# Scores of two attention kinds: bias and mask added by VectorE in the operation that finds the maximum, instead of by TensorE

## The chip, the cores and the metric

The kernel runs on one core of a Trainium2 chip. The metric is the time of one execution in microseconds (us), the median of three runs. Apart from those runs, one execution was profiled; every duration below is from that one.

## What is computed

Two transformer blocks, one after the other, on 256 tokens of width 2048, all in float32. The second block's attention has three kinds of heads, eight of each:

```
diff:  s = q.k * 64**-0.5 - slope[h] * |i - j|, masked by chunks of 64      (two maps for each head)
       w = softmax(s of map 0) - lam * softmax(s of map 1);  o = w v
stick: stick-breaking weights (no softmax)
band:  s = q.k * 64**-0.5 + rel_table[h, clip(i - j)], masked by chunks of 64;  o = softmax(s) v
```

The change touches the scores of the diff heads and of the band heads, and nothing else. The slopes are 2^-1 to 2^-8, one for each diff head.

## The kernel before

**The stream of weights.** Every weight matrix comes in blocks of 128x128, eight to a sub-unit of 512 KB ("sub"). SyncE loads a sub into one of four `raw` buffers (L447), ScalarE rounds it to fp32r into one of five `whi` buffers (L830), VectorE subtracts to make the rest, `wlo` (L1227). TensorE then multiplies each block twice: `whi` with 512 columns (activations as high and low half) and `wlo` with 256. Buffers are given back by semaphores: `sub_done` (TensorE) frees a `whi` buffer, `wlo` (VectorE) frees a `raw` buffer.

**The order.** Four blocks make a "slot"; there are 1860. Everything that is no weight product is a "side task": a generator on each engine, which steps once in each slot, so that the order of every engine's queue is fixed when the program is built. TensorE steps its side tasks after every fourth block. `tasks()` places a diff head (`dfa`, its scores and weights; `dfb`, its output) every 7 slots while the K and the next Q weights stream (v = first slot of stage `ka`: `dfa` h at v+9+7h), and a pair of band heads (`bnd`) at v+117, 127, 135, 143. `BANKS` says in which slots a task holds one of four PSUM banks and which semaphore frees it; `bank_table()` deals them out.

**A diff head before** (`dfa`). TensorE starts both banks (one for each map) with `Ir` x `Dr`, an identity times the table of distances and masks of 384 columns in fp32r, then adds Q x K on top: 128 and 256 columns for each of the two maps, 64 rows deep, in float32, which the trace records as two weight loads and two matmuls each. VectorE takes the maximum of each part (L1458, 128 and 256 columns) and scales it (L1460). ScalarE takes the exponential out of PSUM into SBUF (L1011), with the sum as an accumulator output. VectorE divides and combines the maps (L1463 to L1472, `dif_w`); TensorE transposes three tiles (L649), and `dfb` multiplies with V.

**A pair of band heads before** (`bnd`). TensorE starts each bank with `J` x `hk`: a flip matrix times the head's bias (`HK`), whose rows a DMA read with overlap from a scratch tensor in DRAM, in float32, 128 and 256 columns for each head; then Q x K; then `Ir` x `MCr` in fp32r, the mask of 2 x 64 columns. VectorE's maximum is L1528, ScalarE's exponential L1079, the division L1533 to L1536 (`bnd_w`), the transposes L727.

**The scratch tensor.** In the first block's feed-forward stage, ScalarE's queue loads `c2` (tables) and the 8 rows of the bias, VectorE pads the rows, ScalarE's queue writes the 8 rows of 512 floats to `rel_rows` in DRAM (L985), and after diff head 7 it reads them back as 128 rows of 8 x 256 floats (L1034). ScalarE waits for the write's end before diff head 0, since the diff heads reuse its source.

The lines that follow are of the functions that the change touches.

Of the kernel before, what the change touches and what calls it, by code (L numbers as in the profile page):

```python
# [34 lines left out]
C2 = [("bd", 128), ("tri2", 128), ("flip", 128), ("nm", 384), ("cm", 384), ("dist", 384), ("mc", 64), ("lam", 256)]  # L35
C2_KEPT = 1152
# [173 lines left out]
for _t, _kind, _i in TASKS:  # L210
# [19 lines left out]
    "dfa": [("s0", 2, 5, "dif_exp", 2, 1), ("s1", 2, 5, "dif_exp", 2, 2), ("t", 8, 9, "dif_copy", 1, 1)],  # L230
# [3 lines left out]
    "bnd": [("s0", 2, 6, "bnd_exp", 2, 1), ("s1", 2, 6, "bnd_exp", 2, 2), ("t0", 9, 11, "bnd_copy", 2, 1),  # L234
# [65 lines left out]
def idle(n):  # L300
    for _ in range(n):
        yield
# [3 lines left out]
    "pe_own act_own dve_own pool_own raw0 raw1 raw2 raw3 x0 x1 x2 x3 x4 x5 x6 x7 c1 raw_first whi_first wlo_first scaled vec mem c2 rel rows hank out "  # L306
# [13 lines left out]
class Chip:  # L320


    def __init__(self, nc, ctx, d, out):
# [36 lines left out]
        self.Dr, self.MCr = CR[:, 0:384], CR[:, 384:448]  # L360
# [78 lines left out]
def sync_program(e, c):  # L439
    s = Seq(e, c.sems, "pe_own")  # L440

    def load(w):

        name, i = ORDER[w // 2]
        if w >= NRAW:
            s.wait_ge("wlo", w - NRAW + 1)
        e.dma_start(c.raw[:, w % NRAW, :], c.d[name][i][:, (w % 2) * SUB:(w % 2 + 1) * SUB]).then_inc(c.sems[f"raw{w % NRAW}"], 16)  # L447

    def load_x(i):
        e.dma_start(c.xt(2 * i, 2), c.d["x"][:, 16 + 2 * i * T:16 + (2 * i + 2) * T]).then_inc(c.sems[f"x{i}"], 16)  # L450
# [23 lines left out]
    s.wait_ge("hank", 16)  # L474


def tensor_program(e, c):
# [151 lines left out]
    def dfa(h):  # L629
        yield from idle(2)  # L630
        Q, K = c.Q["a"], c.K["a"]
        p.wait_ge("lam_v", 2)
        p.wait_ge("qk", 10 + 2 * (h // 2))
        banks = [take("dfa", h, f"s{n}") for n in range(2)]
        for bank in banks:
            mm(bank[:, 0:384], c.Ir, c.Dr, True, False)
        for n, bank in enumerate(banks):
            lo, hi = 64 * n, 64 * n + 64
            mm(bank[:, 0:128], Q[lo:hi, h * T:h * T + 128], K[lo:hi, h * T:h * T + 128], False, False)
        for n, bank in enumerate(banks):  # L640
            lo, hi = 64 * n, 64 * n + 64
            p.then_inc(mm(bank[:, 128:384], Q[lo:hi, h * T + 128:(h + 1) * T], K[lo:hi, h * T:(h + 1) * T], False, True),
                       "dif_s")
# [58 lines left out]
    def bnd(i):  # L702
        P0, P1, q = c.bnd[i]
        Q, K, V, J = c.Q["c"], c.K["c"], c.V["c"], c.const2("flip")
        yield from idle(2)
        p.wait_ge("hank", 16)
        p.wait_ge("qk", 30 + 2 * (i // 2))
        banks = [take("bnd", i, f"s{n}") for n in range(2)]
        for n, bank in enumerate(banks):
            hk = c.HK[:, (2 * i + n) * T:(2 * i + n + 1) * T]  # L710
            mm(bank[:, 0:128], J, hk[:, 128:256], True, False)
            mm(bank[:, 128:384], J, hk, False, False)
        for n, bank in enumerate(banks):
# [89 lines left out]
def scalar_program(e, c):  # L803
# [194 lines left out]
    def dfa(h):  # L998
        st = c.SM[:, 16 + 16 * h:32 + 16 * h]
        yield from idle(4)  # L1000
        for n in range(2):
            load(LN_EXP)
            Pb, bank = c.dif[h % 4][n], c.bank("dfa", h, f"s{n}")
            a.wait_ge("dif_max", 2 * h + n + 1)
            if h >= 4:
                a.wait_ge("y_made", made("ao", h - 4))
            else:
                a.wait_ge("norm_ok", 5)
                a.wait_ge("rows", 16)
            for o, w, i in ((0, 128, 0), (128, 256, 1)):  # L1010
                a.then_inc(e.activation(Pb[:, o:o + w], bank[:, o:o + w], ACT.Exp, bias=st[:, 2 * n + i:2 * n + i + 1],  # L1011
                                        scale=SLOPES[h], accum_out=st[:, 4 + 2 * n + i:5 + 2 * n + i]),
                           "dif_exp" if i else None)
        yield from idle(5)
        a.wait_ge("dif_turn", h + 1)
        a.then_inc(e.activation(c.dif[h % 4][0][:, 0:384], c.bank("dfa", h, "t")[:, 0:384], ACT.Copy), "dif_copy")
        yield

    def dfb(h):
# [6 lines left out]
        a.wait_ge("lam_v", 4)  # L1026
# [40 lines left out]
    def bnd(i):  # L1067
# [3 lines left out]
        for n, Pb in enumerate((P0, P1)):  # L1071
            st, bank = c.SM[:, 96 + 16 * (2 * i + n):112 + 16 * (2 * i + n)], c.bank("bnd", i, f"s{n}")
            if i:
                a.wait_ge("y_made", made("ao", 8 + i))
            else:
                a.wait_ge("dif_pv", 8)
# [125 lines left out]
def vector_program(e, c):  # L1202
# [183 lines left out]
    def const(_):  # L1386
# [6 lines left out]
        v.then_inc(e.tensor_copy(c.MCr, c.const2("mc")), "lam_v")  # L1393
# [28 lines left out]
        v.then_inc(e.tensor_copy(g8[:, 319:511], g8[:, 318:319].to_broadcast([8, 192])))  # L1422
        v.then_inc(e.tensor_copy(g8[:, 511:512], g8[:, 318:319]), "fill")
# [26 lines left out]
    def dfa(h):  # L1450
# [3 lines left out]
        for n in range(2):  # L1454
            bank = c.bank("dfa", h, f"s{n}")
# [388 lines left out]
def layout(a):  # L1844
# [71 lines left out]
```

## Time and profile before

| | |
|---|---|
| median of 3 runs | 2743.03 us (2742.43 to 2743.47) |
| the profiled execution | 2743.26 us, of which its span is 2741.3 us |
| TensorE busy | 2717.2 us, 99% of the span |
| VectorE busy | 1949.9 us, 71% |
| ScalarE busy | 1284.8 us, 47% |
| granted TensorE clock, mean | 0.998 |
| DMA | 499 MB, mean 182 GB/s |

Busy is time in which an engine executes; a matmul's record overlaps that of the next one, so a single matmul's cost is best read from one start to the next start. L481 is the helper that issues nearly all matmuls, so they are told apart by tile: `H` or `Y` with `whi` or `wlo` are weight products, `CR` holds `Ir`, `Dr` and `MCr`, and `AR` holds nearly everything else.

### The profile page before, as it was taken

The page shows a single profiled execution, that of the slowest core. Times are in us where ns is not written, and L with a number is a line of the kernel's source. Part 1 is how long each engine was busy: PE and PEld are TensorE (multiplying, and loading weights), DVE is VectorE, ACT ScalarE, POOL GpSimd, SP SyncE. Part 2 cuts the span into 40 slices and gives each one's busy share as a digit, 9 for nine tenths or more (in the row PEclk, how much of TensorE's full clock was granted, in tenths as well). Part 3 has the DMA queues.
Part 4 walks back from the last instruction along what each step waited for, and adds up shares of the span by engine and source line. Part 5 has one row for each costly group of instructions (what it writes and reads, how often), then busy time and mean ns, then how long its engine had stood idle before and what let it go on. Part 6 is the DMA issues. An engine that isn't in the chain of part 4 may idle for free.

```text
span 2741.3 us, 39113 instructions
## 1 busy us (share of the span) xinstructions
PE 2717.2 (99%) x16174; PEld 2378.5 (87%) x16174; DVE 1949.9 (71%) x2378; ACT 1284.8 (47%) x1634; POOL 94.7 (3%) x69
## 2 busy tenths in 40 slices
PE   8999999999999999999999999999999999999998
PEld 7888999888898888888888888888988888888886
DVE  7777777876768665666566886776777757775775
ACT  5444455754545443344344554545544433443444
POOL 1000000011101000000000110000100000000001
PEclk9999999999999999999999999999999999999999
DMA  6555555446555555555555555454455555555553
GB/s 240 191 185 185 175 164 173 145 160 223 182 169 189 187 191 194 191 190 189 190 185 193 191 183 170 150 168 144 164 183 185 200 190 178 193 199 190 187 192 124
DMA packets 138192, 499.07 MB, mean 182 GB/s; under 512 B 15248, under 2 KB 16280, under 8 KB 137888
## 3 DMA queue, kind: packets, MB, share of 16 engines
q1 hardware_dynamic: 136224, 491.67, 54.2%
q10 hardware_dynamic: 1792, 4.91, 0.5%
q8 instruction: 127, 2.08, 0.3%
q14 instruction: 49, 0.40, 0.0%
HBM read 494.41 MB, written 2.11 MB: 181 GB/s over the span
## 4 chain that ended last, share of the span: by engine, by line
PE 98%; DVE 1%; DMA 1%; ACT 0%; POOL 0%; issue 0%; DVEq 0%; ACTq 0%; POOLq 0%
PE PS L481 97%; DMA raw<-in_w_in 0%; DVE wlo L1227 0%; POOL AR L1738 0%; ACT whi L830 0%; DMA XG<-in_x 0%; DVE XG L1677 0%; DVE XG L1210 0%; PE PS L573 0%; DVE H L1221 0%; PE PS L727 0%; PE PS L649 0%; ACT AR L837 0%; PE PS L616 0%; DVEq L1785 0%
## 5 line engine op out<-in xcount | busy, mean ns | idle before, releaser
L481 PE MATMUL PS<-H,whi 128*128 128x512 f32 (+1 forms) x5472 | 1788.9, 381 | 8.7 <-DVE wlo L1705 7.9
L1227 DVE TENSOR_TENSOR wlo<-raw,whi 128x1024 fp32r<-128x1024 f32 x929 | 1127.7, 1231 | 638.5 <-ACT whi L830 634.5
L481 PE MATMUL PS<-H,wlo 128*128 128x256 f32 x5072 | 1412.6, 278 | 0.0
L830 ACT ACTIVATE whi<-raw 128x1024 fp32r<-128x1024 f32 x929 | 969.5, 1057 | 921.2 <-PE PS L481 883.2
L481 PEld LDWEIGHTS PS<-H,whi 128*128 128x128 f32 x5472 | 1001.8, 188 | 220.7 <-issue 8.8
L481 PEld LDWEIGHTS PS<-H,wlo 128*128 128x128 f32 x5072 | 956.3, 189 | 3.5 <-issue 3.1
L481 PE MATMUL PS<-Y,whi 128*128 128x512 f32 (+1 forms) x2240 | 719.0, 376 | 1.1 <-DVE XG L1677 0.8
L481 PE MATMUL PS<-Y,wlo 128*128 128x256 f32 x2048 | 569.3, 278 | 0.0
L481 PEld LDWEIGHTS PS<-Y,whi 128*128 128x128 f32 x2240 | 407.8, 188 | 84.0 <-DVE XG L1677 2.0
L481 PEld LDWEIGHTS PS<-Y,wlo 128*128 128x128 f32 x2048 | 385.6, 188 | 0.5 <-issue 0.2
L1549 DVE TENSOR_REDUCE AR<-PS 128x512 f32<-128x1024 f32 x140 | 171.6, 1225 | 14.6
L1738 POOL TENSOR_TENSOR AR<-AR 128x512 f32<-128x512 f32 x48 | 70.5, 1470 | 2003.8 <-ACT AR L837 2002.8
L815 ACT ACTIVATE AR<-AR 128x512 f32<-128x512 f32 x64 | 40.5, 633 | 211.8 <-DVE AR L1237 138.4
L481 PE MATMUL PS<-whi,H 128*128 128x512 f32 (+1 forms) x384 | 105.0, 361 | 0.0
L1210 DVE TENSOR_TENSOR AR<-AR 128x512 f32<-128x512 f32 x114 | 78.9, 692 | 34.7 <-ACT AR L815 32.3
L481 PE MATMUL PS<-AR 128*128 128x256 f32 (+8 forms) x580 | 99.4, 354 | 2.8 <-ACT AR L837 2.2
L1144 ACT ACTIVATE Y<-AR 128x512 fp32r<-128x512 f32 x44 | 27.8, 632 | 150.0 <-DVE AR L1666 150.0
L1237 DVE SCALAR_TENSOR_TENSOR AR<-AR 128x255 f32<-128x255 f32 (+2 forms) x192 | 92.9, 484 | 6.8
L481 PEld LDWEIGHTS PS<-AR 128*128 128x128 f32 (+3 forms) x580 | 61.5, 170 | 22.4 <-issue 11.6
L481 PEld LDWEIGHTS PS<-whi,H 128*128 128x128 f32 x384 | 67.0, 189 | 10.3 <-issue 1.0
L1219 DVE TENSOR_TENSOR Y<-AR,Y 128x512 fp32r<-128x512 f32 (+1 forms) x68 | 42.7, 628 | 37.4 <-ACT Y L1144 34.5
L481 PE MATMUL PS<-wlo,H 128*128 128x512 f32 (+1 forms) x192 | 68.2, 355 | 0.0
(173 smaller groups left out, 895.6 us busy)
## 6 DMA issues: line engine op xcount, KB each, us to landing
raw<-in_ffn SPq DMA_DIRECT2D x528, 512.0 KB, 4.1
raw<-in_w_in SPq DMA_DIRECT2D x177, 512.0 KB, 4.5
raw<-in_w_qkv SPq DMA_DIRECT2D x96, 512.0 KB, 3.7
raw<-in_w_out SPq DMA_DIRECT2D x64, 512.0 KB, 4.2
raw<-in_w_o SPq DMA_DIRECT2D x40, 512.0 KB, 3.6
raw<-in_w_q SPq DMA_DIRECT2D x8, 512.0 KB, 3.9
raw<-in_w_k SPq DMA_DIRECT2D x8, 512.0 KB, 4.3
raw<-in_w_v SPq DMA_DIRECT2D x8, 512.0 KB, 4.6
```

What stands on the lines that cost most here:

```text
L481: return e.matmul(out, l, r, start=start, stop=stop)
L815: return e.activation(dst, src, ACT.Silu)
L830: a.then_inc(e.activation(c.whi[:, s % NW, :], c.raw[:, s % NRAW, :], ACT.Copy), "whi")
L1144: a.then_inc(e.activation(c.hi("Y", 2 * (j - 8 * part), 2), two(q), ACT.Copy), "y_hi")
L1210: return e.tensor_tensor(two(dst), two(src), both(r), ALU.mult)
L1219: v.then_inc(e.tensor_tensor(c.lo(op, k, n), src, hi, ALU.subtract), made_)
L1227: v.then_inc(e.tensor_tensor(c.wlo[:, s % NW, :], c.raw[:, s % NRAW, :], c.whi[:, s % NW, :].bitcast(F32), ALU.subtract), "wlo")
L1237: v.then_inc(e.scalar_tensor_tensor(dst[:, sh:T], src[:, 0:T - sh], taps(width - 1 - sh), dst[:, sh:T], ALU.mult, ALU.add), name if sh == ...
L1549: v.then_inc(e.tensor_reduce(two(dst), c.acc[b].rearrange("p m (h t) -> p m t h", h=2), AX, ALU.add), f"acc{b}", turn + 1)
L1738: g.then_inc(e.tensor_tensor(c.SUM, c.SUM, c.SQ[i % 2], ALU.add), "sum_add")
```

## The change

In both kinds of heads TensorE now makes Q x K alone. VectorE adds the table and finds the maximum in one `tensor_tensor_reduce`: it reads the bank and the table in SBUF, adds, multiplies by -slope (or -1), writes the negated scores to SBUF and gives out their minimum. For the diff heads the table is the same rounded `Dr`, read as float32; for the band heads it is `BIAS`, in which one operation before pair 0 sets the masked corner. ScalarE's exponential reads SBUF in place, with scale -1, and waits no more for the buffers it overwrites; VectorE takes over those waits. The two score banks are freed by the maximum (slot 4) instead of the exponential (slot 5 or 6); `bank_table()` deals some later banks out differently. The scratch tensor becomes 8 x 128 x 384 floats, each bias row written 128 times, so that the read back can step 383 floats from partition to partition and come out unflipped.

```diff
-    "dfa": [("s0", 2, 5, "dif_exp", 2, 1), ("s1", 2, 5, "dif_exp", 2, 2), ("t", 8, 9, "dif_copy", 1, 1)],
+    "dfa": [("s0", 2, 4, "dif_max", 2, 1), ("s1", 2, 4, "dif_max", 2, 2), ("t", 8, 9, "dif_copy", 1, 1)],
-    "bnd": [("s0", 2, 6, "bnd_exp", 2, 1), ("s1", 2, 6, "bnd_exp", 2, 2), ("t0", 9, 11, "bnd_copy", 2, 1),
+    "bnd": [("s0", 2, 4, "bnd_max", 2, 1), ("s1", 2, 4, "bnd_max", 2, 2), ("t0", 9, 11, "bnd_copy", 2, 1),
...
-        self.HK = AR[:, 3072:5120]
-        self.rows = nc.dram_tensor("rel_rows", [8, 512], F32).ap()
-        self.hank = bass.AP(tensor=self.rows.tensor, offset=0, ap=[[1, P], [512, 8], [1, 256]])
+        self.BIAS = AR[:, 3072:5120]
+        self.rows = nc.dram_tensor("rel_rows", [8, P, 384], F32).ap()
+        self.bias = bass.AP(tensor=self.rows.tensor, offset=127, ap=[[383, P], [384 * P, 8], [1, 256]])
...
     def dfa(h):                                   # TensorE
-        p.wait_ge("lam_v", 2)
         p.wait_ge("qk", 10 + 2 * (h // 2))
         banks = [take("dfa", h, f"s{n}") for n in range(2)]
-        for bank in banks:
-            mm(bank[:, 0:384], c.Ir, c.Dr, True, False)
...
     def bnd(i):                                   # TensorE
-        p.wait_ge("hank", 16)
...
-        for n, bank in enumerate(banks):
-            hk = c.HK[:, (2 * i + n) * T:(2 * i + n + 1) * T]
-            mm(bank[:, 0:128], J, hk[:, 128:256], True, False)
-            mm(bank[:, 128:384], J, hk, False, False)
...
-        for bank in banks:
-            ends = bank.rearrange("p (a b) -> p a b", a=2)[:, :, 64:128]
-            p.then_inc(mm(ends, c.Ir, c.MCr.unsqueeze(1).to_broadcast([P, 2, 64]), False, True), "bnd_s")
...
     def const(_):                                 # ScalarE
-        e.dma_start(c.rows, g8).then_inc(c.sems["rows"], 16)
+        e.dma_start(c.rows, g8[:, 0:384].unsqueeze(1).to_broadcast([8, P, 384])).then_inc(c.sems["rows"], 16)
...
     def dfa(h):                                   # ScalarE
-            Pb, bank = c.dif[h % 4][n], c.bank("dfa", h, f"s{n}")
+            Pb = c.dif[h % 4][n]
             a.wait_ge("dif_max", 2 * h + n + 1)
-            if h >= 4:
-                a.wait_ge("y_made", made("ao", h - 4))
-            else:
-                a.wait_ge("norm_ok", 5)
-                a.wait_ge("rows", 16)
             for o, w, i in ((0, 128, 0), (128, 256, 1)):
-                a.then_inc(e.activation(Pb[:, o:o + w], bank[:, o:o + w], ACT.Exp, bias=st[:, 2 * n + i:2 * n + i + 1],
-                                        scale=SLOPES[h], accum_out=st[:, 4 + 2 * n + i:5 + 2 * n + i]),
+                a.then_inc(e.activation(Pb[:, o:o + w], Pb[:, o:o + w], ACT.Exp, bias=st[:, 2 * n + i:2 * n + i + 1],
+                                        scale=-1.0, accum_out=st[:, 4 + 2 * n + i:5 + 2 * n + i]),
...
     def dfa(h):                                   # VectorE
+            if h >= 4:
+                v.wait_ge("y_made", made("ao", h - 4))
+            else:
+                v.wait_ge("lam_v", 1)
+                v.wait_ge("norm_ok", 5)
+                v.wait_ge("rows", 16)
             v.wait_ge("dif_s", 2 * h + n + 1)
             for o, w, i in ((0, 128, 0), (128, 256, 1)):
-                v.then_inc(e.tensor_reduce(st[:, 2 * n + i:2 * n + i + 1], bank[:, o:o + w], AX, ALU.max, negate=True))
-            v.wait_ge(*v.at)
-            v.then_inc(e.tensor_scalar(st[:, 2 * n:2 * n + 2], st[:, 2 * n:2 * n + 2], SLOPES[h], None, ALU.mult), "dif_max")
+                v.then_inc(e.tensor_tensor_reduce(Pb[:, o:o + w], bank[:, o:o + w], c.dist[:, o:o + w], -SLOPES[h], 3e38,
+                                                  ALU.add, ALU.min, st[:, 2 * n + i:2 * n + i + 1]), "dif_max" if i else None)
...
     def bnd(i):                                   # VectorE
+        if i == 0:
+            v.wait_ge("bias", 16)
+            ends = c.BIAS.rearrange("p (h n) -> p h n", h=8)[0:64, :, 192:256]
+            v.then_inc(e.tensor_scalar(ends, ends, NEG, None, ALU.min), "masked")
...
+            v.wait_ge("masked", 1)
+            if i:
+                v.wait_ge("y_made", made("ao", 8 + i))
+            else:
+                v.wait_ge("dif_pv", 8)
             v.wait_ge("bnd_s", 2 * i + n + 1)
             for o, w, k in ((0, 128, 0), (128, 256, 1)):
-                v.then_inc(e.tensor_reduce(st[:, k:k + 1], bank[:, o:o + w], AX, ALU.max, negate=True), "bnd_max" if k else None)
+                v.then_inc(e.tensor_tensor_reduce(Pb[:, o:o + w], bank[:, o:o + w], bias[:, 256 - w:256], -1.0, 3e38,
+                                                  ALU.add, ALU.min, st[:, k:k + 1]), "bnd_max" if k else None)
```

ScalarE's `bnd` changes as its `dfa` does. The copy of the mask table (`MCr`) on VectorE and two tables of `c2` go as well.

## Rows read from the trace of the kernel before

**Rows 1.** The page: the engines' line, and ScalarE's rounding of the weights.

```profile
PE 2717.2 (99%) x16174; PEld 2378.5 (87%) x16174; DVE 1949.9 (71%) x2378; ACT 1284.8 (47%) x1634; POOL 94.7 (3%) x69
L830 ACT ACTIVATE whi<-raw 128x1024 fp32r<-128x1024 f32 x929 | 969.5, 1057 | 921.2 <-PE PS L481 883.2
```

**Rows 2.** Waits of TensorE, the longest: us in total, times, longest.

```profile
PE PS L481 <- DVE wlo L1705: 7.9, 1, 7.9
```

**Rows 3.** Timeline of TensorE at diff head 0: start, us, what.

```profile
1680.39 0.28 PE L481 MATMUL PS<-H,wlo 128*128 128x256 f32 x1
1680.51 0.52 PE L481 MATMUL PS<-CR 128*128 128x384 f32 x2
1680.96 0.93 PE L481 MATMUL PS<-AR 64*128 64x128 f32 x8
1681.81 0.50 PE L481 MATMUL PS<-H,whi 128*128 128x512 f32 x1
```

**Rows 4.** The same at a stick head pair, whose Q x K has nothing ahead.

```profile
1810.85 0.28 PE L481 MATMUL PS<-H,wlo 128*128 128x256 f32 x1
1811.05 0.93 PE L481 MATMUL PS<-AR 64*128 64x256 f32 x8
1811.91 0.50 PE L481 MATMUL PS<-H,whi 128*128 128x512 f32 x1
1812.25 0.28 PE L481 MATMUL PS<-H,wlo 128*128 128x256 f32 x1
```

**Rows 5.** The same at band pair 2.

```profile
1904.06 0.28 PE L481 MATMUL PS<-Y,wlo 128*128 128x256 f32 x1
1904.18 2.33 PE L481 MATMUL PS<-AR 128*128 128x128 f32 x16
...
1906.99 0.28 PE L481 MATMUL PS<-Y,wlo 128*128 128x256 f32 x1
```

**Rows 6.** Timeline of VectorE, diff head 0, and after band pair 2's maximum.

```profile
1681.86 1.23 DVE L1227 TENSOR_TENSOR wlo<-raw,whi 128x1024 fp32r<-128x1024 f32 x1 [1.17 <-ACT whi L830]
1683.01 0.62 DVE L1458 TENSOR_REDUCE AR<-PS 128x1 f32<-128x128 f32 x2
1684.38 0.17 DVE L1460 TENSOR_SCALAR AR<-AR 128x2 f32<-128x2 f32 x1
1686.56 1.23 DVE L1227 TENSOR_TENSOR wlo<-raw,whi 128x1024 fp32r<-128x1024 f32 x1 [2.01 <-ACT whi L830]
1688.89 0.75 DVE L1472 SCALAR_TENSOR_TENSOR AR<-AR 128x128 f32<-128x128 f32 x2
...
1910.93 1.23 DVE L1227 TENSOR_TENSOR wlo<-raw,whi 128x1024 fp32r<-128x1024 f32 x1 [2.97 <-ACT whi L830]
```

**Rows 7.** Timeline of ScalarE, diff head 0.

```profile
1683.86 0.37 ACT L1011 ACTIVATE AR<-PS,AR 128x128 f32<-128x128 f32 x1 [2.03 <-DVE AR L1460]
1684.12 0.19 ACT L1011 ACTIVATION_READ_ACCUMULATOR AR<-PS,AR 128x1 f32 x1
1684.22 0.47 ACT L1011 ACTIVATE AR<-PS,AR 128x256 f32<-128x256 f32 x1
1684.67 0.36 ACT L1011 ACTIVATE AR<-PS,AR 128x128 f32<-128x128 f32 x1
```

**Rows 8.** Timeline of TensorE and VectorE: transposes of head 0, head 5.

```profile
1690.39 0.49 PE L649 MATMUL PS<-AR 128*128 128x128 f32 x3
...
1752.66 0.75 DVE L1472 SCALAR_TENSOR_TENSOR AR<-AR 128x128 f32<-128x128 f32 x2
...
1753.55 0.52 PE L649 MATMUL PS<-AR 128*128 128x128 f32 x3
```

**Rows 9.** DMA queues, 1790 to 1812 us: packets, MB, share of 16 engines.

```profile
q1 hardware_dynamic: 974, 3.58, 49.1%
q10 hardware_dynamic: 1040, 1.05, 16.0%
```

**Rows 10.** DMA queue, 871 to 873 us: the write of the scratch tensor.

```profile
q10 hardware_dynamic: 16, 0.02, 4.5%
```

More of the change, by code:

```diff
@@ L34 @@
 C1 = [("ident", 128), ("tri", 384), ("mneg", 128)]
-C2 = [("bd", 128), ("tri2", 128), ("flip", 128), ("nm", 384), ("cm", 384), ("dist", 384), ("mc", 64), ("lam", 256)]
-C2_KEPT = 1152
+C2 = [("bd", 128), ("tri2", 128), ("nm", 384), ("cm", 384), ("dist", 384), ("lam", 256)]
 def offsets(table):
@@ L305 @@
 SEMS = (
-    "pe_own act_own dve_own pool_own raw0 raw1 raw2 raw3 x0 x1 x2 x3 x4 x5 x6 x7 c1 raw_first whi_first wlo_first scaled vec mem c2 rel rows hank out "
+    "pe_own act_own dve_own pool_own raw0 raw1 raw2 raw3 x0 x1 x2 x3 x4 x5 x6 x7 c1 raw_first whi_first wlo_first scaled vec mem c2 rel rows bias masked out "
     "whi wlo sub_done acc0 acc1 h_hi h_made y_hi y_made cr "
@@ L473, in sync_program @@
     s.wait_ge("rows", 16)
-    s.wait_ge("hank", 16)
+    s.wait_ge("bias", 16)
 def tensor_program(e, c):
@@ L631, in dfa @@
         Q, K = c.Q["a"], c.K["a"]
[L632 removed]
         p.wait_ge("qk", 10 + 2 * (h // 2))
         banks = [take("dfa", h, f"s{n}") for n in range(2)]
[L635 to L636 removed]
         for n, bank in enumerate(banks):
             lo, hi = 64 * n, 64 * n + 64
[L639 removed]
+            mm(bank[:, 0:128], Q[lo:hi, h * T:h * T + 128], K[lo:hi, h * T:h * T + 128], True, True)
         for n, bank in enumerate(banks):
             lo, hi = 64 * n, 64 * n + 64
[L642 removed]
+            p.then_inc(mm(bank[:, 128:384], Q[lo:hi, h * T + 128:(h + 1) * T], K[lo:hi, h * T:(h + 1) * T], True, True),
                        "dif_s")
@@ L703, in bnd @@
         P0, P1, q = c.bnd[i]
-        Q, K, V, J = c.Q["c"], c.K["c"], c.V["c"], c.const2("flip")
+        Q, K, V = c.Q["c"], c.K["c"], c.V["c"]
         yield from idle(2)
-        p.wait_ge("hank", 16)
         p.wait_ge("qk", 30 + 2 * (i // 2))
@@ L709, in bnd @@
         for n, bank in enumerate(banks):
-            hk = c.HK[:, (2 * i + n) * T:(2 * i + n + 1) * T]
-            mm(bank[:, 0:128], J, hk[:, 128:256], True, False)
-            mm(bank[:, 128:384], J, hk, False, False)
+            lo, hi = 64 * n, 64 * n + 64
+            mm(bank[:, 0:128], Q[lo:hi, i * T:i * T + 128], K[lo:hi, i * T:i * T + 128], True, True)
         for n, bank in enumerate(banks):
             lo, hi = 64 * n, 64 * n + 64
-            mm(bank[:, 0:128], Q[lo:hi, i * T:i * T + 128], K[lo:hi, i * T:i * T + 128], False, False)
-        for n, bank in enumerate(banks):
-            lo, hi = 64 * n, 64 * n + 64
-            mm(bank[:, 128:384], Q[lo:hi, i * T + 128:(i + 1) * T], K[lo:hi, i * T:(i + 1) * T], False, False)
-        for bank in banks:
-            ends = bank.rearrange("p (a b) -> p a b", a=2)[:, :, 64:128]
-            p.then_inc(mm(ends, c.Ir, c.MCr.unsqueeze(1).to_broadcast([P, 2, 64]), False, True), "bnd_s")
+            p.then_inc(mm(bank[:, 128:384], Q[lo:hi, i * T + 128:(i + 1) * T], K[lo:hi, i * T:(i + 1) * T], True, True),
+                       "bnd_s")
         yield from idle(7)
@@ L980, in const @@
         load(LN_EXP)
-        a.wait_ge("lam_v", 3)
+        a.wait_ge("lam_v", 2)
         a.then_inc(e.activation(c.lam[:, 2:4], c.lam[:, 0:2], ACT.Exp), "lam_a")
@@ L1025, in dfb @@
         a.wait_ge("dif_n", h + 1)
-        a.wait_ge("lam_v", 4)
+        a.wait_ge("lam_v", 3)
         root(q[:, T:2 * T], c.bank("dfb", h, "n")[:, 0:T], 1.0 / 128, c.eps_a, "dif_root")
@@ L1033, in dfb @@
             a.wait_ge("rows", 16)
-            e.dma_start(c.HK.rearrange("p (h n) -> p h n", h=8), c.hank).then_inc(c.sems["hank"], 16)
+            e.dma_start(c.BIAS.rearrange("p (h n) -> p h n", h=8), c.bias).then_inc(c.sems["bias"], 16)
         yield
@@ L1071, in bnd @@
         for n, Pb in enumerate((P0, P1)):
[L1072 to L1076, printed above, removed]
+            st = c.SM[:, 96 + 16 * (2 * i + n):112 + 16 * (2 * i + n)]
             a.wait_ge("bnd_max", 2 * i + n + 1)
             for o, w, k in ((0, 128, 0), (128, 256, 1)):
-                a.then_inc(e.activation(Pb[:, o:o + w], bank[:, o:o + w], ACT.Exp, bias=st[:, k:k + 1],
+                a.then_inc(e.activation(Pb[:, o:o + w], Pb[:, o:o + w], ACT.Exp, bias=st[:, k:k + 1], scale=-1.0,
                                         accum_out=st[:, 2 + k:3 + k]), "bnd_exp" if k else None)
@@ L1392, in const @@
         v.then_inc(e.tensor_copy(c.Dr, c.const2("dist")), "lam_v")
-        v.then_inc(e.tensor_copy(c.MCr, c.const2("mc")), "lam_v")
         yield
@@ L1522, in bnd @@
         P0, P1, q = c.bnd[i]
-        yield from idle(3)
-        for n in range(2):
-            st, bank = c.SM[:, 96 + 16 * (2 * i + n):112 + 16 * (2 * i + n)], c.bank("bnd", i, f"s{n}")
+        yield from idle(2)
+        if i == 0:
+            v.wait_ge("bias", 16)
+            ends = c.BIAS.rearrange("p (h n) -> p h n", h=8)[0:64, :, 192:256]
+            v.then_inc(e.tensor_scalar(ends, ends, NEG, None, ALU.min), "masked")
+        yield
+        for n, Pb in enumerate((P0, P1)):
+            st, bank = c.SM[:, 96 + 16 * (2 * i + n):112 + 16 * (2 * i + n)], c.bank("bnd", i, f"s{n}")
+            bias = c.BIAS[:, (2 * i + n) * T:(2 * i + n + 1) * T]
+            v.wait_ge("masked", 1)
[3 more added lines that the diff above has]
+                v.wait_ge("dif_pv", 8)
             v.wait_ge("bnd_s", 2 * i + n + 1)
             for o, w, k in ((0, 128, 0), (128, 256, 1)):
-                v.then_inc(e.tensor_reduce(st[:, k:k + 1], bank[:, o:o + w], AX, ALU.max, negate=True), "bnd_max" if k else None)
+                v.then_inc(e.tensor_tensor_reduce(Pb[:, o:o + w], bank[:, o:o + w], bias[:, 256 - w:256], -1.0, 3e38,
+                                                  ALU.add, ALU.min, st[:, k:k + 1]), "bnd_max" if k else None)
         yield from idle(4)
@@ L1890, in layout @@
     d1 = np.where(ki // 64 <= (qi + P) // 64, -np.abs(qi + P - ki), NEG)
-    mc = np.where(np.broadcast_to(qi < 64, (P, 64)), NEG, 0.0)
     lam = np.concatenate([a[n].reshape(1, 64) for n in ("lambda_q1_2", "lambda_k1_2", "lambda_q2_2", "lambda_k2_2")], axis=1)
     bd = (i[:, None] // 64 == i[None, :] // 64).astype(f)
-    d["c2"] = np.concatenate([bd, le.T, np.eye(P, dtype=f)[::-1], -cm, cm, d0, d1, mc, np.broadcast_to(lam, (P, 256))],
+    d["c2"] = np.concatenate([bd, le.T, -cm, cm, d0, d1, np.broadcast_to(lam, (P, 256))],
                              axis=1).astype(f)
```

7 lines of the change are left out of this document (3 added, 4 removed).

## The prediction

> **What bounds the kernel now.** I read the page first. TensorE is busy for 2717.2 of 2741.3 us, and ScalarE's rounding of the weights sat idle for 921 us, 883 of them until TensorE gave a buffer back [rows 1]: the engines that feed TensorE wait for it, not it for them. The waits of TensorE come next: the longest is 7.9 us, once, at the very start [rows 2], and no wait stands in the stretch of the diff and band heads. So a microsecond of TensorE's queue in that stretch is a microsecond of the whole, as long as nothing there becomes late. Since matmul records overlap, I then read TensorE's timeline from start to start.
>
> **What TensorE no longer does, diff heads.** From the last weight product ahead of a head to the first Q x K matmul is now 1680.96 - 1680.39 = 0.57 us, with the two distance matmuls in it [rows 3]. A stick head's Q x K has nothing ahead of it, and there the same stretch is 1811.05 - 1810.85 = 0.20 us, which includes the change from 128 to 64 rows [rows 4]. Q x K itself is 0.85 us in the one and 0.86 in the other, so it loses nothing when it starts the bank instead of adding to it. Gain: 0.57 - 0.20 = 0.37 us a head, 8 heads, 2.9 us.
>
> **Band heads.** From the last weight product before pair 2 to the second one after it is 1906.99 - 1904.06 = 2.93 us, with flip, Q x K and mask [rows 5]. After the change I build this stretch from the stick pair: 0.20 to Q x K, 0.86 for it, and 0.34 from the first weight product to the second (1812.25 - 1811.91; the weight load is not yet hidden there) [rows 4], 1.40 us in all. Gain 1.53 us a pair, 4 pairs, 6.1 us. The sum is 9.0 us. Where the switch into Q x K costs less than at the stick pair (0.12 us is what lies between a weight product and the next matmul at full rows, rows 3), it is 0.08 x 12 = 1.0 us more.
>
> **What VectorE does instead.** For one map of a diff head it now takes 0.62 us for the two maxima, and with the scaling 0.81 us to the `dif_max` that releases ScalarE; both maps end at 1684.38 + 0.17 = 1684.55, 1.54 us after the start [rows 6]. No row shows a `tensor_tensor_reduce`. Its nearest row is the scalar_tensor_tensor over the same 128 and 256 columns, two tensors in and one out, 0.75 us for both [rows 6]. An accumulator output costs extra on ScalarE: from exponential to exponential is 0.36 us, of which the read of the accumulator adds 0.10 (1684.12 to 1684.22) [rows 7]. Taken over: 0.75 + 2 x 0.10 = 0.95 us a map, 1.90 a head, so 0.36 us more a head; in a band pair, which has no scaling, 1.90 against 2 x 0.62 = 1.24. Below: 0.75 a map, if the read is hidden, which is no more than now. Above: twice the row, 1.5 + 0.2 = 1.7 us a map. I take 0.95, since the operands are as those of that row.
>
> The Trainium skill ("VectorE: DVE Perf Modes", on two Vector instructions with no wait between them) says that an operation which also writes out its accumulator is two instructions, the main one and a read. The trace has no such VectorE operation; ScalarE's rows agree with the rule. By it each `tensor_tensor_reduce` would stand in the trace as two records; without it the sum would be 0.75 us a map, and the predicted time 0.1 us less.
>
> **Does that reach TensorE?** What waits for VectorE is the transpose of the weights (L649). At head 0 the weights are ready at 1688.89 + 0.75 = 1689.64 [rows 6] and the transpose starts at 1690.39 [rows 8]: 0.75 us in hand. The change takes from it twice. First, VectorE's maxima there stand behind a split of weights (1681.86) that was let go by the sub-unit's end just before the distance matmuls [rows 3, 6], so VectorE's chain keeps its place and the transpose comes 0.37 us sooner. Second, the second map's maximum comes at 1683.01 + 1.90 = 1684.91 where ScalarE wanted it at 1684.67 [rows 7]; with the 0.05 us of a semaphore the second exponentials end 0.3 us later, and behind them, in ScalarE's queue, the next `whi`, in VectorE's the next `wlo`, and then the weights. 0.75 - 0.37 - 0.30 leaves 0.08 us: no stall, barely. Head 5 has only 1753.55 - 1753.41 = 0.14 us in hand [rows 8], but its weights follow a `wlo` whose release came after the maxima; VectorE is idle in between, and no distance matmul is removed between that release and the transpose. In a band pair the maxima are followed by an idle of 2.97 us [rows 6], against 0.66 more work. I allow 0.2 us of stall for all heads together.
>
> The waits that move to VectorE (`y_made`, `norm_ok`, `lam_v`, `masked`) are for its own earlier work and cost nothing; `dif_pv` 8 and `rows` were met long before; the wait for `bias` comes 41 slots, some 60 us, after the read is issued. If it did block, the splits of all later weights would queue behind it. The masking operation, 64 partitions by 512 elements, once, and the copy that goes are under 1 us of VectorE, whose queue has 29% of idle time [rows 1]. Freed banks: the wait for `dif_max` or `bnd_max` ends sooner than that for the exponential; TensorE stands in no bank wait now, so nothing is won. ScalarE's exponential reads SBUF instead of PSUM; ScalarE is idle for half of its time.
>
> **The DMAs.** The read back has as many rows of as many bytes as before. The write grows from 16 KB to 8 x 128 x 384 x 4 bytes = 1.57 MB in 1024 packets of 1.5 KB, at about 872 us, while weights stream. In bytes it is three sub-units. The read's packets of 1 KB took 16.0% of 16 engines x 22 us / 1040 = 0.054 us each, weight packets of 4 KB 49.1% x 352 / 974 = 0.177 us [rows 9]; so the write's should take 0.054 to 0.177 us. It may use only 8 engines, since its source has 8 rows (the old write had 8 packets of data, 8 of signals, 0.09 us each: 4.5% of 32 us / 16 [rows 10]). Then an engine gets 128 of them. A sub-unit takes 2741.3 / 930 = 2.95 us and brings each engine 8 weight packets, one in 0.37 us, which leaves 0.19 us beside each: even the dearest of these packets fits, and no weight comes late. Before TensorE stands, lateness must also use up the rounded sub-units ahead, four less ScalarE's 1.06 and VectorE's 1.23 us: 4 x 2.95 - 2.3 = 9.5 us [rows 1, 6]. Cost taken: nothing.
>
> The rule that speaks against the change is in "DMA: Bandwidth & Descriptors" of the Trainium skill, on why a DMA increments its semaphore by 16: a copy is spread over the largest number of engines up to 16 that divides the slowest dimension of both sides, 8 here. Its page "SBUF — State Buffer" (Door 1) puts partitions 0 to 7 on two ports of about 27 GB/s: an estimate by both is 1.57 MB / 54 GB/s = 29 us, 0.23 us a packet, 5 us of lateness, which the 9.5 us would still hide. The old write's packets agree with 8 engines; no row shows the ports' limit.
>
> **The sum.** The profiled execution took 2743.26 us, 0.2 more than the median. 2743.26 - 9.0 + 0.2 = 2734.5; against the median 2743.03 it is 2734.2, 0.32% less.
>
> **Rivals.**
> (a) `tensor_tensor_reduce` at twice its nearest row, 1.7 us a map. Both maps then take 3.4 us; head 0's second exponentials end at about 1683.01 + 3.4 + 0.05 + 0.8 = 1687.3 instead of 1685.5, 1.8 us late, of which 0.38 are in hand. 1.4 us of stall in each of the four heads like head 0, some 0.5 in the others: 6 us, which gives 2734 + 6 = 2740, within 0.2% of before. For it: no row of the operation. Against it: every VectorE row with two tensors in is close to the plain one. Between the two lie 2735 to 2738.
> (b) The scratch write starves the weights. If a packet of it holds its engine for longer than 0.19 + 9.5 / 128 = 0.26 us, TensorE stands; from 0.38 us it eats the whole gain and more than 0.2% besides. At 0.45 us: 128 x 0.26 - 9.5 = 24 us of stall, 2758 us, slower. For it: few partitions read by many engines at once. Against it: the rows' 0.054 to 0.177 us.
> (c) The edit does less than it says: Q x K, now first in its bank, pays the switch and the exposed weight load that the removed matmuls paid. The stick pair's rows already have both in them, so I see at most 0.1 us at each of 12 places: 2735.4.
>
> **How the numbers follow.** The forecast with (c) 0.80, partial stalls up to 2737.5 among it; (a), or another loss of 4 to 9 us, 0.11; (b) 0.07; 0.02 for more gain than 10 us. The forecast's own range is 2733.2 (the 1.0 us above) to 2736.5; for the unknown price of the operation I widen it to 2732.5 to 2738.5, which leaves out (b) and most of (a). 0.2% is 5.5 us, about what a measurement can tell from no change: faster 0.82, same 0.11, slower 0.07.
>
> **What would show it.** TensorE's timeline: 0.20 us from the last weight product to Q x K, 0.86 for it, and no matmul of tile CR behind diff head 0. VectorE: two records each, pairs of 0.95 us a map. Waits of TensorE: none from L649 over 0.3 us, none for `wlo` near 872 to 920 us. The prediction is wrong if the new operation takes over 1.2 us a map, if TensorE waits for `wlo` behind the write, or if the gain per pair is not near 1.5 us.

## The result, and the profile after

The changed kernel takes 2758.59 us (median of 19 runs, 2745.73 to 2760.96); the kernel before takes 2742.98 us (19 runs, 2742.12 to 2743.93). The ratio of the means is 1.0044, 95% interval 1.0036 to 1.0051: slower, where 2734.2 us was forecast. Its runs lie on two levels, 6 at 2745.7 to 2747.6 us and 13 at 2758.3 to 2761.0; the profiled one (2759.13 us, span 2757.3) is of the upper.

The waits of TensorE (us in total, times, longest) against [rows 2]:

```profile
PE PS L480 <- DVE wlo L1207: 9.5, 3, 7.6
PE PS L480 <- DVE wlo L1700: 7.9, 1, 7.9
```

The second row is the old wait at the start. The first is new: TensorE stood for weights. Two of its three waits, 9.1 us together, stand behind the write of the scratch tensor. The timeline of TensorE has the place, and ScalarE's, below it, shows for what ScalarE waited in its turn:

```profile
895.25 0.80 PE L480 MATMUL PS<-H,whi 128*128 128x512 f32 x1 [7.60 <-DVE wlo L1207]
910.49 0.50 PE L480 MATMUL PS<-H,whi 128*128 128x512 f32 x1 [1.52 <-DVE wlo L1207]
```

```profile
892.88 1.06 ACT L819 ACTIVATE whi<-raw 128x1024 fp32r<-128x1024 f32 x1 [12.12 <-DMA raw<-in_ffn]
895.46 1.06 ACT L819 ACTIVATE whi<-raw 128x1024 fp32r<-128x1024 f32 x1 [1.52 <-DMA raw<-in_ffn]
```

The chain is: load late, rounding late, split late, TensorE idle. The write of the scratch tensor was issued at 871.4 us, and its packets ran from 872.9 us on. The DMA view of 874 to 890 us (first line: busy tenths of 16 engines in 40 slices; q10 is ScalarE's queue, here only the write, q1 the weights):

```profile
DMA  4444789844444445899644444448988544444498
GB/s 46 46 50 50 152 241 224 230 50 50 50 46 46 50 50 77 183 244 234 159 46 50 50 50 46 50 46 152 214 204 230 97 50 50 46 50 50 67 188 233
...
q10 hardware_dynamic: 498, 0.76, 43.2%
q1 hardware_dynamic: 252, 0.93, 16.5%
...
raw<-in_ffn SPq DMA_DIRECT2D x4, 512.0 KB, 18.3
```

A packet of the write took 43.2% of 16 engines x 16 us / 498 = 0.22 us, about three times the 0.075 us that lie, for 1.5 KB, between the 1 KB and the 4 KB packets of [rows 9]. In the slices of 46 to 50 GB/s some 40 to 50% of the engines are busy, about 8 of 16, and they move no more than that. The weights got 0.93 MB in 16 us, where 16 / 2.95 sub-units, 2.8 MB, were needed, and a load landed after 18.3 us.

The trace does not name a packet's engine, but the counts tell how the two transfers shared them. First a stretch in which no weights moved (877.4 to 880.2 us), then the one behind it (880.2 to 882.2 us), then all from the write's start to 888.9 us:

```profile
q10 hardware_dynamic: 88, 0.14, 43.6%
```

```profile
q10 hardware_dynamic: 64, 0.10, 44.4%
q1 hardware_dynamic: 72, 0.26, 35.7%
```

```profile
q10 hardware_dynamic: 510, 0.78, 39.3%
q1 hardware_dynamic: 216, 0.79, 12.1%
```

The write keeps its 44% whether weights move or not, so they take nothing from its engines. They come in bursts of 72, which are 64 packets and 8 signals: half of a load, on the other 8 engines. Up to 888.9 us there were three such bursts (216) and nothing else of the weights. Meanwhile each of the write's 8 engines sent 510 / 8 = 64 write packets. A load has landed only when its other half has too, so none landed in that time.

TensorE's clock followed (columns: stretch, length, busy us of PE, PEld, DVE, ACT, POOL with counts, granted clock, DMA share, GB/s):

```profile
884.00:888.00 4.00, 3.65 (x22) 2.94 (x20) 0.00 (x0) 0.00 (x0) 0.00 (x0) 1.00 0.63 114
888.00:892.00 4.00, 0.00 (x0) 0.00 (x0) 0.00 (x0) 0.00 (x0) 0.00 (x0) 0.77 0.67 178
892.00:896.00 4.00, 0.75 (x2) 0.65 (x3) 1.23 (x1) 1.60 (x2) 0.00 (x0) 0.50 0.51 144
896.00:900.00 4.00, 4.00 (x15) 3.43 (x14) 2.17 (x2) 1.57 (x2) 0.00 (x0) 0.50 0.73 207
900.00:904.00 4.00, 4.00 (x24) 3.50 (x24) 2.73 (x3) 1.06 (x1) 0.00 (x0) 0.95 0.63 115
```

It fell to 0.50, the 1.2 GHz level, while TensorE stood, and 15 matmuls fitted into the first 4 us after it started again, instead of 25.

That is not all. I lined up the two traces by the n-th split of weights (every one of 929 is in both). The changed kernel is 12.4 us behind at 934 us, but 25.0 us behind at 1600 us, and in between it waits for nothing. Then it wins 2.7 us in the diff heads and 6.1 us in the band heads, and stays 16.4 us behind to the end. Between 934 and 1600 us its matmuls simply come at a slower rhythm. The row of before and then that of after, both at full clock:

```profile
1200.00:1300.00 100.00, 100.00 (x579) 87.44 (x578) 67.01 (x64) 42.91 (x46) 0.00 (x0) 1.00 0.57 190
```

```profile
1200.00:1300.00 100.00, 100.00 (x569) 86.79 (x568) 65.98 (x63) 41.03 (x45) 0.00 (x0) 1.00 0.57 187
```

569 matmuls against 579 in 100 us is 1.8% slower; over the 690 us from 910 to 1600 us that makes 12 us. From start to start, a pair of weight products (one of `whi`, one of `wlo`) takes 350 and 343.5 ns by turns in the faster rhythm (346.7 on average), and 349, 350 and 361 in the slower one (353.3), each repeated with hardly a break.

The part that was forecast came out. Diff head 0 after the change, to be held against [rows 3]:

```profile
1705.44 0.28 PE L480 MATMUL PS<-H,wlo 128*128 128x256 f32 x1
1705.65 0.93 PE L480 MATMUL PS<-AR 64*128 64x128 f32 x8
1706.51 0.51 PE L480 MATMUL PS<-H,whi 128*128 128x512 f32 x1
```

From weight product to Q x K is 0.21 us instead of 0.57. And the new VectorE operation, against [rows 6]:

```profile
1708.05 0.28 DVE L1442 CUSTOM_DVE_ANT_0 AR<-PS,CR 128x128 f32<-128x128 f32 x1
1708.26 0.08 DVE L1442 DVE_READ_ACCUMULATOR2_ANT AR<- 128x1 f32 x1
1708.26 0.42 DVE L1442 CUSTOM_DVE_ANT_0 AR<-PS,CR 128x256 f32<-128x256 f32 x1
...
1709.16 0.09 DVE L1442 DVE_READ_ACCUMULATOR2_ANT AR<- 128x1 f32 x1
```

Both maps take 1709.25 - 1708.05 = 1.20 us, less than the 1.54 before; the read of the accumulator runs beside the next operation.

### The profile page after: what moved, and what is told of

The parts are those of the page before. It is cut to its first block, busy times and chain, and to the rows that moved or that the text cites. A ratio compares the mean times of both kernels' runs of the same rounds, so it can differ in the third digit from the quotient of the medians.

```text
span 2757.3 us, 39029 instructions
## 1 busy us (share of the span) xinstructions
PE 2723.4 (99%) x16118; PEld 2380.5 (86%) x16118; DVE 1947.8 (71%) x2409; ACT 1286.1 (47%) x1634; POOL 94.8 (3%) x69
## 4 chain that ended last, share of the span: by engine, by line
PE 94%; DVE 2%; DMA 2%; ACT 1%; POOL 0%; issue 0%; DVEq 0%; ACTq 0%; POOLq 0%
PE PS L480 94%; DMA raw<-in_ffn 1%; DVE wlo L1207 1%; ACT whi L819 1%; DVE XG L1407 0%; DMA raw<-in_w_in 0%; POOL AR L1733 0%; DVE AR L1544 0%; DMA XG<-in_x 0%; DVE XG L1672 0%; DVE XG L1190 0%; PE PS L572 0%; DVE H L1201 0%; PE PS L716 0%; PE PS L645 0%
## 5 line engine op out<-in xcount | busy, mean ns | idle before, releaser
L480 PE MATMUL PS<-AR 128*128 128x256 f32 (+9 forms) x548 | 93.3, 355 | 2.8 <-ACT AR L826 2.2
```

Of the source, the lines that this page charges most:

```text
L480: return e.matmul(out, l, r, start=start, stop=stop)
```

## The experiments

Times are medians, each kernel beside runs of the kernel before on the same chip (2742.9 to 2743.2 us); ratios are of the means. The diffs are shortened to the lines that matter. Experiments 1, 3 and 4 leave out the right content of the bias and serve for the time alone.

**1. The change without the big write.**

```diff
-        self.rows = nc.dram_tensor("rel_rows", [8, P, 384], F32).ap()
-        self.bias = bass.AP(tensor=self.rows.tensor, offset=127, ap=[[383, P], [384 * P, 8], [1, 256]])
+        self.rows = nc.dram_tensor("rel_rows", [8, 384], F32).ap()
+        self.bias = bass.AP(tensor=self.rows.tensor, offset=0, ap=[[1, P], [384, 8], [1, 256]])
-        e.dma_start(c.rows, g8[:, 0:384].unsqueeze(1).to_broadcast([8, P, 384])).then_inc(c.sems["rows"], 16)
+        e.dma_start(c.rows, g8[:, 0:384]).then_inc(c.sems["rows"], 16)
```

> The changed kernel, but the scratch tensor is 8 x 384 floats and written once (12 KB instead of 1.57 MB); the read back goes over it with step 1, so that the bias of the band heads comes out mirrored. Theory (the big write starves the weights, and the stop of TensorE that follows leaves it at a slower pace): TensorE never waits for wlo after the start, the pair of weight products stays at 346.7 ns on average between 960 and 1560 us, all runs lie within 1 us of each other, and the time is 2743.0 - 8.9 = 2734.1 us. Rival (the slower pace comes from the new VectorE operation or from the changed order of instructions, not from the write): the pace stays at 353 ns and the time is about 2747 us or has two levels.

Measured: 2734.03 us (2733.49 to 2734.74, 5 runs), ratio 0.9967 (0.9954 to 0.9979). Its only wait of TensorE between 860 and 1640 us:

```profile
PE PS L480 <- DVE AR L1544: 0.4, 1, 0.4
```

It comes after the stretch of the slow rhythm and stands in the changed kernel too. The pace is 579 matmuls from 1200 to 1300 us. All else of the change together gains 9.2 us; the big write, and what follows from it, costs 12 us on the lower level and 25 on the upper.

**2. The write without the change.**

```diff
+        e.dma_start(c.extra, g8[:, 0:384].unsqueeze(1).to_broadcast([8, P, 384])).then_inc(c.sems["extra"], 16)
```

> The kernel before, with the write of 8 x 128 x 384 floats added to it, into a tensor of its own that nobody reads; all else as before. Theory: the weights starve as in the changed kernel, TensorE stops for 7 to 8 us near 888 us and once more for some 1.5 us, its clock goes to the lower level for some 13 us, 12 to 13 us in all: 2756 us where the pace stays at 346.7 ns a pair, 2768 us where it goes to 353 ns up to 1600 us; both levels show over the rounds. Rival (the stop is special to the changed kernel): 2743 to 2745 us.

Measured: 2768.7 us (2767.8 to 2770.62, 4 runs), ratio 1.0095 (1.008 to 1.0111). TensorE's waits behind the write (9.0 us against 9.1) and the write's packets (874 to 890 us) are close to those of the changed kernel:

```profile
PE PS L483 <- DVE wlo L1231: 9.0, 2, 8.3
```

```profile
q10 hardware_dynamic: 497, 0.76, 43.1%
q1 hardware_dynamic: 244, 0.90, 17.1%
```

The upper level was forecast at 2768; the lower one did not show in 4 runs. The write is to blame, with or without the rest of the change, and no VectorE operation.

**3. The same bytes from 128 partitions.**

```diff
+        e.dma_start(c.rows.rearrange("h p n -> p h n"), c.rel[:, 0:384].unsqueeze(1).to_broadcast([P, 8, 384])).then_inc(c.sems["rows"], 16)
```

> The changed kernel, but the big write takes its 1024 packets of 1.5 KB from 128 partitions (eight packets from each) instead of 8; the bytes and the target stay, the content of the bias is another. Theory A (the few source partitions hold each packet for 0.22 us): the packets take well under 0.15 us, spread over 16 engines, the write is over in about 10 us, TensorE does not wait for wlo, 2734 us. Rival B (writes of 1.5 KB to DRAM are that slow wherever they come from): 0.22 us again, 64 on each of 16 engines, over in some 20 us, TensorE stops for a few us, 2737 to 2750 us.

Measured: 2734.14 us (2733.77 to 2734.8, 5 runs). The DMA view of 872 to 880 us:

```profile
GB/s 0 0 138 369 369 376 369 369 376 369 369 361 369 376 369 369 376 369 369 361 376 300 230 192 259 213 305 287 410 307 307 369 287 164 123 225 328 164 225 246
...
q10 hardware_dynamic: 1040, 1.57, 56.9%
```

The first slices, at up to 376 GB/s, are nearly all the write's. A packet took 56.9% x 128 us / 1040 = 0.07 us, and all 1.57 MB were over in less than 8 us. Writing 1.5 KB packets to DRAM is not slow. TensorE did not wait.

**4. Again 8 partitions, but 0, 4, 8 to 28.**

```diff
+        e.dma_start(c.rows, c.rel[0:32:4, 0:384].unsqueeze(1).to_broadcast([8, P, 384])).then_inc(c.sems["rows"], 16)
```

> The changed kernel, but the 8 source partitions are 0, 4, 8 to 28 instead of 0 to 7; packets, bytes, target and the number of source rows stay, the content of the bias is another. Theory A1 (what holds the packets is that 8 neighbouring partitions share a path out of SBUF): packets fall to 0.06 to 0.12 us, the write takes under 18 us, TensorE waits for wlo less than 2 us, 2734 to 2737 us. Rival A2 (what counts is that only 8 DMA engines work, at any place of the source): packets stay at 0.22 us, and the stop of 7 us stays, 2746 or 2759 us.

Measured: 2734.14 us (2733.97 to 2734.5, 5 runs), and TensorE has no wait at all between 860 and 1640 us. The write's first 3 us (872.6 to 875.6 us), in which no weights moved:

```profile
q10 hardware_dynamic: 375, 0.58, 50.7%
```

These are again 8 of 16 engines, but they move 0.58 MB in 3 us, 192 GB/s, at 50.7% x 48 us / 375 = 0.065 us a packet. So it is where the 8 partitions lie that makes a packet dear, not that there are 8, nor that 8 engines work. The Trainium skill ("SBUF — State Buffer", Door 1) puts 0 to 7 on two ports and 0, 4 to 28 on eight. The traces agree with it: 46 to 50 GB/s for the one, below the 54 that the page's 27 a port give for two (an estimate), and packets of a third of the length for the other.

**5. The write as it is, in 16 pieces.**

```diff
+        for n in range(16):
+            e.dma_start(c.rows[:, 8 * n:8 * n + 8, :], g8[:, 0:384].unsqueeze(1).to_broadcast([8, 8, 384])).then_inc(c.sems["rows"], 16)
+            yield from idle(4)
```

> The changed kernel whole, but its big write goes out in 16 pieces of 8 copies, five slots (some 7 us) apart, from the same 8 partitions. Packets stay at 0.22 us; each piece gives each of 8 engines 8 of them, 1.8 us. Theory (only the write's length in one piece does the harm): no wait for wlo after the start, pace 346.7 ns, 2734.1 us, all runs on one level. Rival (some lateness per piece adds up, or the write costs by its bytes): over 2736 us.

Measured: 2734.64 us (2734.07 to 2735.24, 5 runs), ratio 0.9969 (0.9957 to 0.9981); loads land after 4.7 us from 870 to 990 us, and TensorE waits for no weights there. The slow source does no harm when its packets come in small groups: 8 of them hold an engine for 8 x 0.22 = 1.8 us.

**6. The whole change, the bias rows on partitions 0, 4 to 28.** The load, the padding (over 32 partitions) and the write move there.

```diff
-        e.dma_start(g8[:, 127:319], c.d["rel"]).then_inc(c.sems["rel"], 16)
+        e.dma_start(c.rel[0:32:4, 127:319], c.d["rel"]).then_inc(c.sems["rel"], 16)
...
+        e.dma_start(c.rows, c.rel[0:32:4, 0:384].unsqueeze(1).to_broadcast([8, P, 384])).then_inc(c.sems["rows"], 16)
```

> The changed kernel whole, with the 8 bias rows loaded to, padded on and written from partitions 0, 4 to 28 instead of 0 to 7, in one piece. Packets 0.065 us as in spread_source, write over in some 14 us, 2734.1 us. Rival (the earlier run was fast because its content differed): 2746 or 2759 us.

Measured: 2734.07 us (2733.75 to 2734.5, 4 runs), ratio 0.9967 (0.9954 to 0.998). This version beats both kernels. The write from 872 to 890 us, and band pair 2 on TensorE:

```profile
q10 hardware_dynamic: 1032, 1.57, 24.1%
```

```profile
1898.06 0.28 PE L480 MATMUL PS<-Y,wlo 128*128 128x256 f32 x1
...
1899.46 0.28 PE L480 MATMUL PS<-Y,wlo 128*128 128x256 f32 x1
```

A packet took 24.1% x 288 us / 1032 = 0.067 us. The stretch of the band pair is 1899.46 - 1898.06 = 1.40 us, as forecast, against 2.93 in [rows 5].

**7. A shorter write.** 96 of 128 copies at once, the rest in four pieces later.

```diff
+        e.dma_start(c.rows[:, 0:96, :], g8[:, 0:384].unsqueeze(1).to_broadcast([8, 96, 384])).then_inc(c.sems["rows"], 16)
+        for n in range(4):
+            yield from idle(60)
+            e.dma_start(c.rows[:, 96 + 8 * n:104 + 8 * n, :], g8[:, 0:384].unsqueeze(1).to_broadcast([8, 8, 384])).then_inc(c.sems["rows"], 16)
```

> The changed kernel, but the first piece of the write is 96 of 128 copies, and the other 32 follow in four small pieces 60 slots apart. Theory (lateness grows with the length of the piece; four write packets to one weight packet on each shared engine): the first piece lasts some 25 us, lateness is three quarters, so TensorE stops for 1 to 4 us instead of 9, with no or a short fall of its clock; 2735 to 2739 us, or some 12 us more if a short stop is enough to bring the slower pace. Rival (the stop is a matter of any large write): 2746 or 2759 us as before.

Measured: 2755.77 us (2742.79 to 2757.62, 10 runs), again on two levels. The size of the stop was missed: in the profiled run (2744.97 us, lower level) TensorE waited 7.2 us for `wlo`, with the fall of its clock.

```profile
PE PS L480 <- DVE wlo L1210: 7.2, 1, 7.2
```

The first stop is all but the 7.6 us of the whole write; what is gone is the second, of 1.5 us. Lateness does not grow in proportion. From 871 to 888.4 us the two queues look as in the changed kernel:

```profile
q10 hardware_dynamic: 517, 0.79, 41.1%
q1 hardware_dynamic: 216, 0.79, 13.3%
```

Again three bursts of weights and 517 / 8 = 65 write packets an engine. A write of 96 packets an engine is as long as one of 128 for whoever gets no turn before the first 64. This also refutes the four to one that I expected: no fixed share fits both these 16 us and the time behind them. This run has the stop and the fallen clock and yet 579 matmuls from 1200 to 1300 us, so a stop can also leave the fast rhythm in place.

**8. A stop alone.** In the kernel before, one more 16 KB write, and TensorE waits for it at the slot of its issue. The first lines are TensorE's side task, the last two ScalarE's, behind its write of the rows.

```diff
+    def const(_):
+        yield from idle(30)
+        p.wait_ge("extra", 16)
+        yield
...
+        yield from idle(13)
+        e.dma_start(c.extra, g8).then_inc(c.sems["extra"], 16)
```

> The kernel before, with a write of 16 KB to a tensor of its own in the same stage and a wait of TensorE for it at the slot of its issue: one stop of some 2 us and nothing else. Theory C (any stop can switch TensorE's rhythm): some or all runs at the slower pace of 353 ns until about 1600 us, 2743 + 2 + 12 = 2757 us beside 2745 us. Rival D (it takes the fall of the clock): pace 346.7 ns in all, 2745 us on one level.

Measured: 2756.81 us (2743.67 to 2761.39, 6 runs), ratio 1.0045. In the profiled run the stop was 0.6 us, with the clock at 1.00, and the rhythm behind it was the slow one:

```profile
PE PS L483 <- DMA extra_rows<-AR: 0.6, 1, 0.6
```

```profile
1200.00:1300.00 100.00, 100.00 (x568) 86.77 (x567) 66.18 (x63) 40.79 (x44) 0.00 (x0) 1.00 0.56 186
```

That run is 13.4 us over the kernel before, of which 0.6 us is the standing. Of the other five, four lie at 2756.6 to 2761.4 us and one at 2743.67; how long they stood was not profiled. The slow rhythm does not take the fall of the clock.

**9. The control: the same instructions, the wait ten slots later.**

> As pause_only, but TensorE's wait stands ten slots (some 14 us) later, so that the 16 KB write has long landed: the same instructions and the same DMA, no stop. Theory C (the stop itself switches the rhythm): 2743 us, one level, 346.7 ns a pair. Rival (the added wait or DMA does it, stop or not): 2756 us in part of the runs, as in pause_only.

Measured: 2742.95 us (2742.59 to 2743.74, 11 runs), ratio 1.0001 (0.9992 to 1.001). TensorE does not stand at the added wait, and the rhythm behind it is the fast one:

```profile
1200.00:1300.00 100.00, 100.00 (x579) 87.44 (x578) 67.05 (x64) 42.84 (x46) 0.00 (x0) 1.00 0.56 190
```

So it is not the added wait or DMA, but the standing.

**10. The stop at 1350 us.**

> As pause_only, but write and wait come 336 slots later, near 1350 us instead of 883 us. Theory C (a rhythm that lasts from the stop to the next stage's side work near 1600 us, 1.9% slower all the while): the slower level is 2743 + 0.6 + 250 x 0.019 = 2748 us, some runs stay at 2743 to 2744 us. Rival (a fixed cost of 12 us for the stop): 2756 us.

Measured: 2748.73 us (2744.57 to 2749.8, 11 runs), ratio 1.0018 (1.0009 to 1.0026). The stop in the profiled run was 1.8 us; the rhythm before and behind it:

```profile
1200.00:1300.00 100.00, 100.00 (x579) 87.46 (x578) 67.37 (x64) 42.53 (x46) 0.00 (x0) 1.00 0.57 190
1400.00:1500.00 100.00, 100.00 (x568) 86.69 (x567) 65.67 (x63) 41.23 (x45) 0.00 (x0) 1.00 0.55 185
```

The profiled run (2748.82 us) is 5.9 us over the kernel before, not 12: the price goes by the time left to 1600 us. Runs between the two levels (2746.3 twice, 2747.2) were not foreseen; how long each of them stood wasn't profiled.

**11. Two stops, near 883 and 1160 us.**

> As pause_only, with a second 16 KB write and wait 200 slots after the first, near 1160 us. Theory C, if each stop deals the rhythm anew: three or four levels, 2744 (both fast), 2749 (slow up to 1160 us), 2752 (slow from there), 2757 us (slow throughout). Rival C1 (the first stop fixes it, the slow rhythm outlasts further stops): the levels of pause_only, 2744 and 2757 us, and 0.6 us more.

Measured: 2754.83 us (2746.96 to 2766.93, 6 runs). In the profiled run (2753.57 us) TensorE stood 0.3 us at the first and 2.8 us at the second. It went slow at the first and fast again at the second:

```profile
PE PS L483 <- DMA extra_rows<-AR: 3.1, 2, 2.8
```

```profile
1000.00:1100.00 100.00, 100.00 (x568) 86.79 (x567) 59.65 (x57) 38.34 (x38) 0.00 (x0) 1.00 0.56 189
1200.00:1300.00 100.00, 100.00 (x579) 87.42 (x578) 66.80 (x63) 42.05 (x47) 0.00 (x0) 1.00 0.56 190
```

So a later stop can also end the slow rhythm, and rival C1 falls. The levels were missed: for this order 2749 us was forecast. The second stop was longer than planned, and the clock was at 0.59 in the 4 us behind it. One run at 2766.93 us lies above every level that I named; its mean clock, 0.996, is the lowest of the six (0.997 and 0.998), but it has no profile and stays open.

## Why the prediction was wrong

- **The gain on TensorE, 9.0 us: right.** 9.2 us without the big write, 8.8 to 9.1 with it from another source, 8.3 with it in pieces. Diff heads 2.7 (2.9 forecast), band heads 6.1 (6.1). Nothing was hidden or given back in the heads.
- **VectorE's price, 0.95 us a map: too dear.** 0.60. The read of the accumulator is a record of its own, as the page of the Trainium skill named in the prediction ("VectorE: DVE Perf Modes", on two Vector instructions with no wait between them) says, but lies beside the next operation. No transpose waited; rival (a) is out, and so is the 0.2 us of stall. Rival (c) is out with the 0.21 us of the switch. Rival (a)'s own terms were added wrongly: four heads at 1.4 us and four at 0.5 make 7.6 us, not 6; nothing hangs on it now.
- **The step that failed is "Cost taken: nothing" for the DMAs**, in two of its terms: the price of a packet and the sharing of the engines. The next two points take them one by one.
- **First, the packet.** I took 0.054 to 0.177 us from reads and weight loads, all of which touch 128 partitions. It measured 0.22, because 8 neighbouring source partitions let out 46 to 50 GB/s in all (experiments 3, 4 and 6). One row did start from partitions 0 to 7, the old write of [rows 10], and I misread it: 0.09 us is the average of 8 data packets and 8 signals. Singly, in the packed trace, the data packets of 2 KB took 0.17 us on average and the signals 0.01. From 872.37 to 872.72 us, the stretch in which they ran, the queue view of before reads:

```profile
DMA packets 16, 0.02 MB, mean 47 GB/s; under 512 B 8, under 2 KB 8, under 8 KB 16
```

That is the rate of the big write. My estimate from the two ports of the Trainium skill, 0.23, was right, and I kept it out of the sum.
- **Second, the sharing.** I gave every weight packet its turn after each write packet. Until 888.9 us the weights got no turn on the write's engines, for 16 us and 64 write packets on each. Only then did it go nearly by turns: the four loads that hung landed at 892.9, 895.4, 897.9 and 900.3 us, and beside their 32 packets an engine each engine sent some 40 of the write. By turns alone, 0.22 us a packet would have cost 128 x (0.22 - 0.19) = 4 us of lateness, which the reserve hides; that is why I had put the point at 0.26. The reserve of 9.5 us did not cover 16 us without a turn, and 9.1 us of standing came on top.
- **Rival (b)** named the outcome, but its condition, a packet over 0.26 us, was not met, and the 24 us it priced came by another sum. Why the write sends 64 packets on each engine before the weights get a turn, no run here shows.
- **What no step had: what a stop leaves behind.** The 9.1 us of standing had become 12.4 us by 934 us, most of the rest being the clock at 0.50. Then comes the rhythm, some 12.6 us more. Both levels follow: 2743.0 - 9 + 12.4 = 2746 (2745.7 to 2747.6 measured, 6 of 19 runs), and 12.6 more is 2759 (2758.3 to 2761.0, 13 runs). No run of the changed kernel on its lower level was profiled; that such a run keeps the fast rhythm is taken from the profiled run of experiment 7. Experiments 8 to 11 show that a stop can set the rhythm, that the added instructions do not, and that it lasts to the next stage or the next stop. What holds it, and what decides which one a stop leaves, is open; it is not the length alone, for stops of 0.3, 0.6 and 1.8 us left the slow one, and stops of 2.8 and 7.2 us the fast one, but the changed kernel's 7.6 and 1.5 us the slow one.

## What to carry to other kernels

A transfer is not priced by bytes and packet size alone: look at how many partitions it touches and where they lie, and test it against the reserve of the stream that it runs beside, with the unkind assumption that the stream gets no turn for a while (here 64 packets an engine). When an average over a queue's packets is taken, take the signals out first. A one-off DMA of a setup stage can cost more than the loop that it serves gains; spread its rows over the partitions, or send it in pieces. And where a kernel's gain is bought on an engine that never stands, the first stop anywhere may cost a multiple of its length (here 13 us for 0.6), so look for new waits in the whole trace before judging the edit itself.

## What the runs showed of the hardware

- 8 source partitions side by side (0 to 7): 1.5 KB packets of 0.22 us, 46 to 50 GB/s. The same 8 rows at 0, 4 to 28: 0.067 us, 192 GB/s on 8 engines. 128 partitions: 0.07 us on 16 engines, up to 376 GB/s.
- The write's 8 engines took no weight packet before they had sent 64 packets of the write, 16 us; a 512 KB load took 18 us instead of 4 to 5. That 8 engines are meant is worked out from counts and shares.
- TensorE at full granted clock has two lasting rhythms for the same alternation of 512 and 256 columns: 346.7 and 353.3 ns a pair, 579 and 568 matmuls in 100 us. A stop of 0.3 or 0.6 us can bring the slow one, one of 2.8 us ended it.
- `tensor_tensor_reduce` with one operand in PSUM takes 0.28 us for 128 and 0.42 us for 256 columns, as much as the plain maximum (0.62 us for both), and its accumulator read 0.08 us beside the next operation.
